# State-space stage of a two-block kernel: one product kept in the PSUM banks, its matmuls moved behind two projection steps, one buffer more for the decay rows and one fewer for y

## The reference

```python
lam_bar = jnp.exp(lam * dt[:, None])
b_bar = ((lam_bar - 1.0) / lam)[..., None] * bmat
bu = jnp.einsum('btgs,gps->btgp', u_chunk.astype(jnp.complex64), b_bar)
# x_t = lam_bar * x_(t-1) + bu_t   (a scan over the 256 context and then the 512 latent tokens)
y = jnp.einsum('btgp,gsp->btgs', xs, cmat).real
...
y = jax.nn.gelu(y.astype(g.dtype))
ya, yb = jnp.split(y @ w_glu + b_glu, 2, axis=-1)
return ((ya * jax.nn.sigmoid(yb)) * jax.nn.silu(g)) @ w_out
```

## Time and profile before

| what | us |
|---|---|
| median of 3 runs | 2220.47 (2219.76 to 2221.86) |
| the profiled execution's own time | 2218.46 |
| its span, first to last instruction | 2216.7 |
| S5's quads, from the first L2925 to the last L2950 | 1358.5 to 1662.6 |

### The profile page before, as it was taken

One profiled execution on the slowest core, in us unless ns is written; L12 is line 12 of the kernel. 1 busy time (PEld: TensorE's weight loads), 2 busy tenths in 40 slices (PEclk: granted clock), 3 DMA queues, 4 the chain that ended last, 5 costly groups with the idle time before them and its releaser, 6 DMA issues.

```text
span 2216.7 us, 38909 instructions
## 1 busy us (share of the span) xinstructions
PE 2086.7 (94%) x15596; PEld 1510.8 (68%) x15596; DVE 1271.0 (57%) x1896; ACT 766.5 (35%) x1425; POOL 632.0 (29%) x1129
## 2 busy tenths in 40 slices
PE   7999898999998999999989978999979999999997
PEld 6887777755554555555556547888867788888785
DVE  3366664459994444444467766999992333333334
ACT  3335543231103444444410036544444332222223
POOL 2643111500016888888701211111121000000000
PEclk9999999999999999999999989999999999999999
DMA  9221443423452111111135425999964233323321
GB/s 359 83 88 60 145 154 124 161 79 121 164 180 86 53 53 53 53 55 70 53 143 212 164 79 151 299 301 297 291 206 150 86 96 97 102 96 95 96 86 38
DMA packets 119411, 292.42 MB, mean 132 GB/s; under 512 B 11616, under 2 KB 57056, under 8 KB 113088
## 3 DMA queue, kind: packets, MB, share of 16 engines
q1 hardware_dynamic: 107072, 226.10, 31.4%
q0 software_dynamic: 12160, 63.84, 7.8%
HBM read 223.97 MB, written 65.93 MB: 131 GB/s over the span
## 4 chain that ended last, share of the span: by engine, by line
PE 82%; DVE 10%; issue 3%; ACT 3%; POOL 1%; DMA 0%; SPq 0%; DVEq 0%; ACTq 0%; POOLq 0%
PE psum L470 29%; PE psum L1867 8%; PE psum L2563 7%; PE psum L2306 5%; PE psum L2342 5%; PE psum L2737 4%; PE psum L2317 3%; PE psum L1142 3%; PE psum L2331 2%; PE psum L2387 2%; PE psum L2378 2%; DVE early L2937 2%; PE psum L304 2%; DVE early L2917 2%; DVE const L2950 1%
## 5 line engine op out<-in xcount | busy, mean ns | idle before, releaser
L470 PE MATMUL psum<-split,w_split 128*128 128x512 f32 x1632 | 371.5, 389 | 0.0
L470 PEld LDWEIGHTS psum<-split,w_split 128*128 128x128 f32 x1632 | 306.3, 188 | 63.7
L452 DVE TENSOR_TENSOR w_split<-ring,w_split 128x512 fp32r<-128x512 f32 x182 | 129.0, 709 | 309.3 <-ACT w_split L447 308.9
L2088 POOL TENSOR_TENSOR early<-early 128x8 f32<-128x8 f32 (+6 forms) x672 | 277.6, 413 | 52.8
L447 ACT ACTIVATE w_split<-ring 128x512 fp32r<-128x512 f32 x182 | 115.1, 633 | 337.0 <-PE psum L470 334.0
L1867 PE MATMUL psum<-early,ring 128*128 128x512 f32 (+1 forms) x544 | 176.5, 486 | 0.0
L2563 PE MATMUL psum<-gate,ring 128*128 128x512 f32 (+1 forms) x512 | 165.4, 486 | 1.2 <-issue 1.2
L2737 PE MATMUL psum<-h,u_w 128*128 128x256 f32 (+1 forms) x768 | 151.7, 349 | 15.1 <-ACT u_t L2651 11.4
L1867 PEld LDWEIGHTS psum<-early,ring 128*128 128x128 f32 x544 | 103.7, 191 | 71.8 <-issue 64.7
L2563 PEld LDWEIGHTS psum<-gate,ring 128*128 128x128 f32 x512 | 97.2, 190 | 69.3 <-issue 62.7
L470 PE MATMUL psum<-h,w_split 128*128 128x512 f32 x552 | 134.5, 404 | 8.0 <-DVE w_split L452 8.0
(11 more groups left out here) (439 smaller groups left out, 3511.9 us busy)
## 6 DMA issues: line engine op xcount, KB each, us to landing
ring<-in_s_glu SPq DMA_DIRECT2D x64, 512.0 KB, 3.5
ring<-in_w_mod SPq DMA_DIRECT2D x48, 512.0 KB, 5.8
made_c_pow<-area POOLq DMA_DIRECT2D x16, 1152.0 KB, 5.0
c_pow<-made_c_pow SPq DMA_DIRECT2D x32, 576.0 KB, 5.3
ring<-in_s_in SPq DMA_DIRECT2D x32, 512.0 KB, 6.4
made_b_pow<-area POOLq DMA_DIRECT2D x15, 1024.0 KB, 4.5
b_pow<-made_b_pow SPq DMA_DIRECT2D x15, 1024.0 KB, 10.2
ring<-in_w_in SPq DMA_DIRECT2D x25, 512.0 KB, 3.6
```

Of the source, the lines that this page charges most:

```text
L452: nc.vector.tensor_tensor(rounded(buffer(u, 1)), source(u), buffer(u, 0), ALU.subtract).then_inc(dve_done, 1)
L470: ins = nc.tensor.matmul(out, rounded(buffer(u, w)[:, ks]), values(x, k), start=(first and k == 0 and n == 0), stop=(last and k == UNIT_K ...
L2088: nc.gpsimd.tensor_tensor(o, a, b, op).then_inc(pool_done, 1)
```

## The change

1. `state_dve`: the sine product comes first, into `mod_s`. The cosine product is written over x in the PSUM banks themselves. The add and the subtraction take their first operand from the banks and write `mod_c`. "x_read" is marked behind the subtraction.
2. `s5_pe`: each quad begins with two projection steps (k = 0, 1 or 4, 5) ahead of `x_pe`; one step stands behind each `turn_pe` (2, 3 or 6, 7).
3. `decay` has two buffers, so `decay_act` waits for the scans of two quads before. It stands at the head of ScalarE's quad.
4. `y_out` has one buffer, so `y_turn_act(m)` waits until the store of tile m-1 has landed. It waited for tile m-2.

```diff
-        y_out = early_part(2048, 1024).rearrange("p (b t) -> p b t", b=2)
+        y_out = early_part(2048, 512)
...
-        decay = sb(s5, "decay", [4, C_ALL])
+        decay = [sb(s5, "decay", [4, C_ALL]), early_part(6272, 4 * C_ALL).rearrange("p (g c) -> p g c", g=4)]
...
         def decay_act(act, q):
-            if q >= 1:
-                act.wait_ge(*at("s5", "scanned", q - 1))
+            if q >= 2:
+                act.wait_ge(*at("s5", "scanned", q - 2))
...
-            v.tensor_tensor(mod_c, x, both_parts(0, 0, C_ALL), ALU.mult).then_inc(dve_done, 1)
+            v.tensor_tensor(mod_s, x, both_parts(1, 0, C_ALL), ALU.mult).then_inc(dve_done, 1)
             dve_count.up()
-            tt(mod_s, x, both_parts(1, 0, C_ALL), ALU.mult, "s5", "x_read", q)
-            v.tensor_tensor(mod_c[:, 0, :, :], mod_c[:, 0, :, :], mod_s[:, 1, :, :], ALU.add).then_inc(dve_done, 1)
+            tt(x, x, both_parts(0, 0, C_ALL), ALU.mult)
+            v.tensor_tensor(mod_c[:, 0, :, :], x[:, 0, :, :], mod_s[:, 1, :, :], ALU.add).then_inc(dve_done, 1)
             dve_count.up()
-            tt(mod_c[:, 1, :, :], mod_c[:, 1, :, :], mod_s[:, 0, :, :], ALU.subtract)
+            tt(mod_c[:, 1, :, :], x[:, 1, :, :], mod_s[:, 0, :, :], ALU.subtract, "s5", "x_read", q)
...
         def y_turn_act(act, m):
             act.wait_ge(*at("s5", "y_turned", m))
-            if m >= 2:
-                act.wait_ge(y_stored[m % 2], 16 * (m // 2))
-            nc.scalar.activation(y_out[:, m % 2, :], bank(Y_TURN_BANK),
+            if m >= 1:
+                act.wait_ge(*ready(y_stored, m - 1))
+            nc.scalar.activation(y_out, bank(Y_TURN_BANK),
                                  ACT.Gelu_apprx_tanh).then_inc(act_done, 1)
...
-        TOKENS = (((0, 1, 2), (3, 4)), ((5,), (6, 7)))
+        STEPS_FIRST = ((0, 1), (4, 5))
+        STEPS_BEHIND = (((2,), (3,)), ((6,), (7,)))
...
             for q in range(QUADS):
                 m, h = divmod(q, TILE_QUADS)
+                for k in STEPS_FIRST[h]:
+                    u_project_pe(pe, m + 3, k)
                 x_pe(pe, q + 1)
...
             for q in range(QUADS):
                 m, h = divmod(q, TILE_QUADS)
+                decay_act(act, q + 1)
                 if h == 0 and m > 0:
                     y_turn_act(act, m - 1)
...
                 else:
                     lags_act(act, m + 1)
-                decay_act(act, q + 1)
                 y_act(act, q)
```

More of the change, by code:

```diff
@@ L2614, in build @@
         lag_m = early_part(0, 2048).rearrange("p (b g c) -> p b g c", b=2, c=P)
-        y_out = early_part(2048, 1024).rearrange("p (b t) -> p b t", b=2)
-        y_tm = early_part(3072, 1024).rearrange("p (s c) -> p s c", s=STEP)
-        b_pow_t = early_part(4096, 1024).rearrange("p (b j c) -> p b j c", b=2, c=P)
-        s5_tmp = early_part(5120, 16 * C_ALL)
+        y_out = early_part(2048, 512)
+        y_tm = early_part(2688, 1024).rearrange("p (s c) -> p s c", s=STEP)
+        b_pow_t = early_part(3712, 1024).rearrange("p (b j c) -> p b j c", b=2, c=P)
+        s5_tmp = early_part(4736, 16 * C_ALL)
         b_bar_split = early_part(B_SPLIT, 4 * TPD * GS).rearrange("p (r t e i) -> p r t e i", r=2, t=TPD, e=2)
@@ L2682, in s5_start_dve @@
             rest(KD - 1)
-            v.memset(decay[:, :, 0:1], 0.0).then_inc(dve_done, 1)
+            v.memset(decay[0][:, :, 0:1], 0.0).then_inc(dve_done, 1)
+            dve_count.up()
+            v.memset(decay[1][:, :, 0:1], 0.0).then_inc(dve_done, 1)
             dve.wait_ge(dve_done, dve_count.up("s5", "decay_zero"))
@@ L2875, in decay_act @@
                 return
-            if q >= 1:
-                act.wait_ge(*at("s5", "scanned", q - 1))
+            if q >= 2:
+                act.wait_ge(*at("s5", "scanned", q - 2))
             for g in range(4):
-                nc.scalar.activation(decay[:, g, 1:C_ALL], mask("ones")[:, 1:C_ALL], ACT.Copy,
+                nc.scalar.activation(decay[q % 2][:, g, 1:C_ALL], mask("ones")[:, 1:C_ALL], ACT.Copy,
                                      scale=decay8[:, 4 * q + g:4 * q + g + 1]).then_inc(act_done, 1)
@@ L2936, in state_dve @@
                 line = lambda ap: ap[:, ri, :, :].rearrange("p g c -> p (g c)")
-                v.tensor_tensor_scan(line(zs), decay[:, :, :].rearrange("p g c -> p (g c)"), line(mod_c), 0.0,
+                v.tensor_tensor_scan(line(zs), decay[q % 2][:, :, :].rearrange("p g c -> p (g c)"), line(mod_c), 0.0,
                                      ALU.mult, ALU.add).then_inc(dve_done, 1)
@@ L3026, in s5_pe @@
                     turn_pe(pe, 2 * q + 4 + n)
-                    for k in TOKENS[h][n]:
+                    for k in STEPS_BEHIND[h][n]:
                         u_project_pe(pe, m + 3, k)
@@ L3084, in s5_pool @@
                 pool.wait_ge(y_stored[i], 16 * KE // 2)
-            nc.gpsimd.memset(y_out[:, 0, 0:1], 0.0).then_inc(pool_done, 1)
+            nc.gpsimd.memset(y_out[:, 0:1], 0.0).then_inc(pool_done, 1)
             pool.wait_ge(pool_done, pool_count.up("s5", "y_stored"))
@@ L3089, in y_store_pool @@
             pool.wait_ge(*at("s5", "yT", m))
-            pool.dma_start(io["y"][m], y_out[:, m % 2, :]).then_inc(y_stored[m % 2], 16)
+            pool.dma_start(io["y"][m], y_out).then_inc(y_stored[m % 2], 16)
         FIRST_LAST = KE - 7
```

## The result

| what | before | after |
|---|---|---|
| median, four runs each on one chip | 2220.85 us (2219.76 to 2221.86) | 2203.57 us (2202.76 to 2205.21) |
| profiled execution, its span | 2218.46, 2216.7 | 2205.21, 2203.4 |
| VectorE busy over the span | 1271.0 | 1241.9 |

The ratio is 0.9923, with an interval of 0.9906 to 0.994: faster by 17.3 us where 9.3 were forecast, outside the range. The two profiled executions are 13.25 apart. The one of before is 2.4 under its median and 1.3 under the lowest of its four runs; the one of after is 1.6 over its median and the highest of its four. That makes the other 4, so the traces have to explain 13.25.

What follows compares the result with a forecast made beforehand. A ring of waits across TensorE, ScalarE and VectorE, 18.91 us a tile, was taken as the bound. Gains 9.0 + 1.2 - 0.9 = 9.3 us from 2218.46, plus 2.0 for the median, gave 2211.2 us; range 2207 to 2218.

Steps and rivals of the forecast that it cites:

- What bounds the kernel: S5's first nine tiles: a ring of waits of 18.91 us a tile that neither VectorE (17.78 own work) nor TensorE fills.
- head start: TensorE's lags in S5 come 1.3 us before VectorE asks; falling back 0.28 a tile uses this up in four to five tiles.
- the term: S5's tiles behind 1528 us: removing the decay wait there gains another 1.2 us, with little more to be had.
- TensorE's own work: S5: 18.06 us a tile without waits, unchanged when one projection step moves from the even to the odd quad.
- the first part: S5's first nine tiles: VectorE's waits go, gaining 10.2 us, less 1.2 for TensorE falling behind: 9.0.
- Waits and cover: S5: decay wait (0.60 a tile) and `x_pe` wait (0.42) go; two steps ahead of `x_pe` cover the later bank release.
- the later mark: "x_read" behind the subtraction: costs nothing with two steps ahead of `x_pe`; without them about 1.05 us a quad.
- The lag wait: VectorE's wait for ScalarE's lag copy in S5, 0.55 us a tile, goes with 1.3 to spare.
- The product in the banks: VectorE's product written to PSUM in S5: taken to cost nothing, at most about 0.8 us a quad.
- The rival of a dear write: Writing the product into PSUM costs up to 0.8 us in each of 32 quads: slower, 2234.7 us; chance 0.08.
- One y buffer: New ring of gelu, store issue and landing, 17.8 us at median landing 5.4; cost taken as 0.9 in nine tiles.
- Transfers: Rival: DMA share 0.93 is already the limit, loads land later, tiles stay at 18.91: 2219.3 us; chance 0.14.

Runs made afterwards that it cites:

- experiment 1: Kernel before, with GpSimd rounding only 8 of 512 columns of S5's half weights from the third tile on: 2195.23 us, ratio 0.9885.
- experiment 9: Kernel before, with each GpSimd rounding held until VectorE has finished `x_in` of the quad it is in, nothing else: 2202.87 us, ratio 0.993.
- experiment 10: Kernel of experiment 9, with ScalarE's decay rows also moved ahead of the second `turn_act`, still one decay buffer: 2196.41 us, ratio 0.9894 to the kernel before.
- Experiment 2: Kernel before, with only the product written into the PSUM banks and the banks released behind the subtraction: 2236.29 us, ratio 1.0069.
- Experiment 11: Kernel after, with each GpSimd rounding held until the scans of VectorE's own quad are through: 2315.01 us, ratio 1.0429 to the kernel before.
- experiment 4: Kernel before, with only the two decay buffers, decay rows at the head of ScalarE's quad and one y buffer: 2210.55 us, ratio 0.996.

## Why the prediction was right in direction and wrong in size

**What bounds the kernel: the step that failed.** "Its own work is thus 18.91 - 1.13 = 17.78 a tile." I took all busy time of VectorE as its own work. It held two stalls of 1.0 to 1.1 us a tile, each inside the duration of an `x_in`. From the trace after: one quad is 7.88, less 0.25 of wait, and the other 10.54, less 2.42: 15.75 a tile; the first tile, without any wait, takes 15.83. That is 2.0 under my figure, and experiments 1 and 9 show the cause, by removing the rounding and by moving it. The number was in reach: the four `x_in` of a quad together took 2.56 us where four medians make 1.7, and the chain had 1.29 us of "issue" in the middle of them.

**What follows from it.** With VectorE at 15.75, TensorE alone is the bound once its head start is used up, even at the 18.06 that I gave it. Later tiles, which I gave 1.2 because VectorE was "busy 95.1 of 99.0", gained 7.7: part of that busy time was stall. That is 6.5 more than the term, less 1.0 in the first nine tiles: 14.8 for S5 and not 9.3. Of the 8.0 between 17.3 and 9.3 the other 2.5 are the 4 between medians and profiled executions, less the 1.5 given back outside S5.

**TensorE's own work: mis-sized twice.** I took 18.06 and kept it, "the sum stays". The old order's own work is 17.77, as experiment 10 shows, where it runs without waits: 18.06 held 0.29 that was not work. And the new order needs 18.42. The rows of experiment 10 let the 0.65 between the two be added up. Eight steps take 8.94 in four groups there (3.25, 2.26, 1.14, 2.29) and 9.27 in six after (2.28, 1.14, 1.22, 2.28, 1.13, 1.22): 0.33. `x_pe` takes 1.42 behind `y_pe` and 1.48 behind a step, twice: 0.12. From `y_pe` to what follows it is 1.36 when that is `x_pe` and 1.46 when it is a step, twice: 0.20. The end of `y_pe` and what follows it, first in experiment 10, then after:

```profile
1523.15 0.39 PE L2971 MATMUL psum<-early,u_t 128*64 128x128 f32 x4
1523.37 1.49 PE L2907 MATMUL psum<-u_t,early 128*64 128x96 f32 x32
```

```profile
1518.85 0.39 PE L2973 MATMUL psum<-early,u_t 128*64 128x128 f32 x4
...
1519.17 2.36 PE L2739 MATMUL psum<-h,u_w 128*128 128x256 f32 x12
```

Where it is lost is thus shown; why a change from one kind of matmul to another costs it, no run tells. Over nine tiles the first part gained 7.1 where 8.1 (9.0 less 0.9) were forecast. That the two are near is luck: from the third tile on a tile gives 0.5 and not 0.9, and the first tile, which my sum treated like the others, gives 3.0.

**Waits and cover: right.** The decay wait, the wait of `x_pe` for the banks and that of `y_pe` for `x_in` are gone from the first nine tiles. Experiment 2 takes the cover away, and the later mark costs 1.06 a tile: the size as stated, but once a tile and not "a quad", since only the `x_pe` of the even quad waits for the banks. The lag wait "goes" was wrong: VectorE, now the faster, waits for it 2.4 a tile, and it costs nothing.

**The product in the banks: right.** 956 ns against 948, some 8 ns a quad, 0.3 us in all. The rival of a dear write is out. What I had not seen is what it gives: a product, an add and a subtraction that GpSimd doesn't hold up.

**One y buffer: right as a mechanism, too dear in the sum.** Taken at 0.9; the gelu waited for a store 5.5 us in two of sixteen tiles, with no such wait in the tile that is shown. Landings had a median of 4.6. Experiment 11 shows the same ring as the bound once the store is issued later.

**Transfers: out.** At a DMA share of 0.92 a tile takes 18.42, and 17.77 in experiment 10, at 0.93.

**The rival that I had not named** is that the order of TensorE's steps moves an operation on GpSimd, two queues away. The prediction follows the moved steps to `x_pe`, to the lags and to the gelu, and nowhere asks what the rounding would stand beside. It is chance that experiment 4, which has only the decay wait removed and the stall left, comes out where I forecast the whole change.

**What stays open:** why TensorE's boundaries cost what they do, and the 4 us between the difference of the medians and of the profiled executions. I put them down to the spread of the runs, which is not shown.

## What to carry to other kernels

Before a busy time is taken as an engine's own work, look at the minimum, median and maximum of each form: a maximum of three medians can be a stall that shows in no list of waits. When a list on one engine is reordered, follow what it releases through every queue behind it, and ask what each shared resource is doing at its new place. And try the cheapest move alone: here one wait on GpSimd gave what a four-part change gave.

## What the runs showed of the hardware

- A VectorE instruction with two SBUF operands that is issued during GpSimd's 1.3 us subtraction (128x512, two SBUF sources) finishes only after it: `x_in` 1.5 in place of 0.42, the add 1.14 in place of 0.56, a 128x512 product 1.76 in place of 0.69. The time is inside its duration. With one of its two operands in PSUM it is not held up: 0.96 beside the rounding and 0.96 without it (experiment 9).
- It goes the other way too. In experiment 11 nearly every rounding starts 0.06 to 0.10 us after a VectorE product with two SBUF operands; it takes 1.73 in the median (1.59 to 1.77) against 1.29 in experiment 9's first nine tiles, and that product keeps its 0.69.
- A VectorE product of 768 fp32 elements a partition written over its own PSUM source takes 956 ns, written to SBUF 948.
- TensorE's projection steps of six matmuls take 1.08 each in a group of three (experiment 10), and 1.13 to 1.22 alone.
